# Last block of a three-block transformer step: index keys and attention keys and values projected as one tile of 328 columns, and another table of hooks

## The reference, cut to what matters

```python
SPLITS = (ATTN_WIDTH, KV_WIDTH, KV_WIDTH, IDX_HEADS * IDX_DIM, IDX_DIM, IDX_HEADS, D_RNN, D_RNN, D_MODEL, D_MODEL)
#         q 512       k 128     v 128     qi 512               ki 64    wi 8       xr 1024 yr 1024 gate_a   gate_b
dots = jnp.einsum('bqhd,bsd->bqhs', qib, k_idx) * (IDX_DIM ** -0.5)
score = jnp.einsum('bqh,bqhs->bqs', wb * (IDX_HEADS ** -0.5), jax.nn.relu(dots))
_, sel = lax.top_k(where(causal, score, -inf), n_sel)          # 64 of 256 keys for each query
logits = q . k[sel] + rel_bias ; p = softmax(logits) ; o = p @ v[sel]     # 8 heads, 2 key/value heads
rnn = rg_lru(conv(xr), w_rg, b_rg, w_ig, b_ig, lru_lambda) * gelu(yr)     # linear recurrence over 256 steps
merged = sigmoid(gate_a) * dot(attn, w_o_attn) + sigmoid(gate_b) * dot(rnn, w_o_rnn)
```

## Time and profile before

| | us |
|---|---|
| median of 3 runs | 1084.23 (1083.28 to 1085.28) |
| the profiled execution | 1086.36 |
| its span, first to last instruction | 1084.3 |
| TensorE matmul busy | 1026.4 (95%) |
| VectorE busy | 732.6 (68%) |
| ScalarE busy | 585.8 (54%) |
| GpSimd busy | 115.6 (11%) |
| DMA | 213.98 MB, mean 197 GB/s |

### The profile page before, as it was taken

The page is one execution under the profiler, slowest core; times in us unless marked ns, Lnnn a source line. Parts: engine busy times, 40 slices in busy tenths (PEclk is TensorE's granted clock), DMA queues, the critical chain, the costliest instruction groups (busy, mean ns, idle before and its releaser), DMA issues.

```text
span 1084.3 us, 13459 instructions
## 1 busy us (share of the span) xinstructions
PE 1026.4 (95%) x5180; PEld 850.1 (78%) x5180; DVE 732.6 (68%) x986; ACT 585.8 (54%) x842; POOL 115.6 (11%) x168
## 2 busy tenths in 40 slices
PE   6897999999999989899999999997999999999996
PEld 4675878889888777788888878886877788888885
DVE  5567775566346577578888666769766765777753
ACT  6657554444335567544443354577656456676641
POOL 0112140000000022200000011013630000000001
PEclk9999999999999999999999989999999999999998
DMA  9765479555556432389999796535465535554431
GB/s 348 274 170 73 136 202 303 188 181 174 194 175 197 157 113 76 101 287 352 353 325 320 295 317 215 166 121 165 147 213 206 163 112 184 191 193 156 175 136 39
DMA packets 98190, 213.98 MB, mean 197 GB/s; under 512 B 5440, under 2 KB 12880, under 8 KB 94736
## 3 DMA queue, kind: packets, MB, share of 16 engines
q1 hardware_dynamic: 93424, 196.39, 53.2%
q0 software_dynamic: 4416, 16.51, 6.3%
q10 hardware_dynamic: 288, 0.23, 0.1%
HBM read 208.39 MB, written 6.15 MB: 198 GB/s over the span
## 4 chain that ended last, share of the span: by engine, by line
PE 73%; DVE 11%; ACT 8%; issue 4%; DMA 2%; POOL 1%; SPq 0%; DVEq 0%; ACTq 0%; POOLq 0%
PE bank L883 22%; PE bank L885 22%; PE bank L884 22%; ACT hi L1199 4%; DVE lo L1634 4%; PE bank L861 3%; PE bank L898 1%; PE bank L863 1%; ACT junk L1062 1%; DMA raw<-in_w_in_a 1%; DVE early L1465 1%; DVE xres L1508 1%; DMA raw<-in_w_gate_up 1%; DMA early<-in_memT 1%; PE bank L944 0%
## 5 line engine op out<-in xcount | busy, mean ns | idle before, releaser
L1634 DVE TENSOR_TENSOR lo<-raw,hi 128x2048 fp32r<-128x2048 f32 (+1 forms) x164 | 366.9, 2240 | 215.7 <-ACT hi L1199 215.1
L1199 ACT ACTIVATE hi<-raw 128x2048 fp32r<-128x2048 f32 (+1 forms) x164 | 303.7, 1855 | 184.2 <-PE bank L885 144.0
L883 PE MATMUL bank<-hi,xTh 128*128 128x512 f32 (+2 forms) x896 | 346.8, 387 | 2.6 <-DVE lo L1634 2.2
L885 PE MATMUL bank<-hi,xTl 128*128 128x512 f32 (+2 forms) x896 | 337.7, 377 | 0.0
L884 PE MATMUL bank<-lo,xTh 128*128 128x512 f32 (+2 forms) x896 | 337.7, 377 | 0.0
L883 PEld LDWEIGHTS bank<-hi,xTh 128*128 128x128 f32 x896 | 170.6, 190 | 33.7 <-DVE lo L1634 2.8
L885 PEld LDWEIGHTS bank<-hi,xTl 128*128 128x128 f32 x896 | 170.2, 190 | 31.7
L884 PEld LDWEIGHTS bank<-lo,xTh 128*128 128x128 f32 x896 | 170.5, 190 | 28.5
L883 PE MATMUL bank<-hi,hTh 128*128 128x512 f32 x264 | 103.5, 392 | 0.2 <-DVE lo L1634 0.2
L885 PE MATMUL bank<-hi,hTl 128*128 128x512 f32 x264 | 102.8, 389 | 0.0
L884 PE MATMUL bank<-lo,hTh 128*128 128x512 f32 x264 | 102.8, 389 | 0.0
(11 more groups left out here) (346 smaller groups left out, 1315.2 us busy)
## 6 DMA issues: line engine op xcount, KB each, us to landing
raw<-in_w_gate_up SPq DMA_DIRECT2D x44, 1024.0 KB, 6.4
raw<-in_w_down SPq DMA_DIRECT2D x30, 1024.0 KB, 5.1
raw<-in_w_ada SPq DMA_DIRECT2D x24, 1024.0 KB, 6.2
raw<-in_w_up SPq DMA_DIRECT2D x22, 1024.0 KB, 5.1
raw<-in_w_in SPq DMA_DIRECT2D x21, 1024.0 KB, 5.0
raw<-in_w_out SPq DMA_DIRECT2D x12, 1024.0 KB, 5.1
raw<-in_w_in_b SPq DMA_DIRECT2D x10, 1024.0 KB, 5.1
raw<-in_w_in_a SPq DMA_DIRECT2D x6, 1024.0 KB, 11.9
```

The source lines that it names most:

```text
L883: e.matmul(o, sh, h[:, k, :], start=p.first and k == 0, stop=False)
L885: done = e.matmul(o, sl, h[:, k, :], start=False, stop=p.last and k == p.nk - 1)
L1199: e.activation(hi_s[m % SPLITS][:, 0:n], raw[p.at % RAWS][:, 0:n], ACT.Copy).then_inc(hi_made, 1)
L1634: e.tensor_tensor(lo_s[s][:, 0:n], raw[p.at % RAWS][:, 0:n], hi_s[s][:, 0:n].bitcast(F), ALU.subtract).then_inc(lo_made, 1)
```

## The change

**One tile for two.** The tiles `kw` (index key and index weights, 72 columns, second in the table) and `kv` (keys and values, 256 columns, eighth) become one tile `kvw` of 328 columns, second in the table. The host reorders the columns of `w_in_2` and `b_in_2`, so that they are neighbours. The copies that doubled the keys for two heads of a pair (lines 1589 and 1595) are gone: the bias additions read their operand twice. The index key gets its own buffers, those of the first probability slot. Transposes `ki` and `kv` now wait for the whole bias addition of `kvw`.

**Another table of hooks.** The steps behind the queries' tile are laid over four tiles instead of five. `scan0` and `scan1` come later relative to the tiles, `rec1` comes ahead of `top6` and `top7`, `half1` and `bias1` come ahead of `s2`.

```diff
-IN2 = [("qi", 768, 512, ["", "", ""]),
-       ("kw", 1280, 72, ["qi0", "qi2", "x1"]),
-       ("xr", 1352, 512, ["ki", "h0", ""]),
+IN2 = [("qi", 512, 512, ["", "", ""]),
+       ("kvw", 1024, 328, ["qi0", "qi2", "x1"]),
+       ("xr", 1352, 512, ["ki", "h0", "kv"]),
        ("yr", 2376, 512, ["conv00", "h2 conv02", "h4"]),
        ("xr", 1864, 512, ["gelu00", "gelu02 h6", "gate000 gate002 top"]),
        ("yr", 2888, 512, ["gate010 gate012 top0", "conv10 top1", "rec0"]),
-       ("q", 0, 512, ["conv12 top2", "gelu10 inc0 top3", "gelu12 scan0"]),
-       ("kv", 512, 256, ["top4", "half0 bias0 q0 gate100 top5", "q2 gate102 gate110 gate112"]),
-       ("gb", 4424, 512, ["kv top6 top7", "rec1 mask", "attend inc1 s0"]),
-       ("gb", 4936, 512, ["s1 scan1", "s2", "half1 bias1"]),
-       ("ga", 3400, 512, ["", "s3", "s4"]),
-       ("ga", 3912, 512, ["s5", "s6", "s7"])]
+       ("q", 0, 512, ["conv12 top2", "gelu10 inc0 top3", "gelu12 top4"]),
+       ("gb", 4424, 512, ["scan0 q0", "half0 bias0 q2 gate100 gate102", "top5 gate110 gate112"]),
+       ("gb", 4936, 512, ["rec1 top6 top7", "mask attend inc1", "scan1 s0"]),
+       ("ga", 3400, 512, ["s1", "half1 bias1 s2", "s3"]),
+       ("ga", 3912, 512, ["s4", "s5", "s6 s7"])]
...
+        kiT = [x[:, 0, :] for x in p_slots[2][0]]
...
                 elif kind == "ki":
-                    e.wait_ge(kw_dup, 2)
-                    turned(claim(step), blocks_of(staged2_slot("kw"), 128, 1))
+                    e.wait_ge(acc_dve, in2_tile[1024].d1)
+                    turned(claim(step), blocks_of(staged2_slot("kvw"), 384, 1))
                 elif kind == "kv":
-                    e.wait_ge(kv_dup, 4)
-                    turned(claim(step), blocks_of(staged2_slot("kv"), 256, 2))
+                    e.wait_ge(acc_dve, in2_tile[1024].d1)
+                    turned(claim(step), blocks_of(staged2_slot("kvw"), 0, 2))
...
-                elif kind == "in2" and l == "kv":
-                    s = staged2_slot("kv")
+                elif kind == "in2" and l == "kvw":
+                    s = staged2_slot("kvw")
                     e.wait_ge(acc_dve, t_.d1)
-                    e.activation(v[2][0][:, :, :], s[:, :, 128:256], ACT.Copy).then_inc(v2_high, 1)
+                    e.activation(v[2][0][:, :, :], s[:, :, 256:384], ACT.Copy).then_inc(v2_high, 1)
...
-                if what == "kw":
-                    e.wait_ge(acc_dve, t_.d1)
-                    e.tensor_scalar(wi[:, :, :], s[:, :, 64:72], 8.0 ** -0.5, None, ALU.mult).then_inc(wi_made, 1)
-                    for u in range(2):
-                        e.tensor_copy(s[:, :, 128 + 64 * u:192 + 64 * u], s[:, :, 0:64]).then_inc(kw_dup, 1)
-                elif what == "kv":
...
+            def project_keys(t_, pair, full, s, row):
+
+                def twice(x, heads):
+                    return x.rearrange("p (h d) -> p h d", h=heads).unsqueeze(2).to_broadcast([128, heads, 2, 64])
+
+                for t in range(2):
+                    e.wait_ge(*full[t])
+                    e.tensor_tensor(s[:, t, 384:512].rearrange("p (h u d) -> p h u d", h=1, u=2), twice(pair[t][:, 256:320], 1), twice(row[:, 256:320], 1), ALU.add)
+                    e.tensor_tensor(wi[:, t, :], pair[t][:, 320:328], row[:, 320:328], ALU.add).then_inc(wi_sum, 1)
+                    e.tensor_tensor(s[:, t, 0:256].rearrange("p (h u d) -> p h u d", h=2, u=2), twice(pair[t][:, 0:128], 2), twice(row[:, 0:128], 2), ALU.add)
+                    e.tensor_tensor(s[:, t, 256:384], pair[t][:, 128:256], row[:, 128:256], ALU.add).then_inc(acc_dve, 1)
+                e.wait_ge(wi_sum, 2)
+                e.tensor_scalar(wi[:, :, :], wi[:, :, :], 8.0 ** -0.5, None, ALU.mult).then_inc(wi_made, 1)
+                e.wait_ge(v2_high, 1)
+                e.tensor_tensor(v[2][1][:, :, :], s[:, :, 256:384], v[2][0][:, :, :].bitcast(F), ALU.subtract).then_inc(v2_low, 1)
```

More of the change, by code:

```diff
@@ L431, in named @@
     def named(self, name):
-        for kind in ("conv", "gelu", "qi", "ki", "kv", "top", "half", "bias", "rec", "inc", "scan", "gate", "q", "h", "s"):
-            if name.startswith(kind) and name not in ("kv", "ki", "top"):
+        for kind in ("conv", "gelu", "qi", "top", "half", "bias", "rec", "inc", "scan", "gate", "q", "h", "s"):
+            if name.startswith(kind) and name != "top":
                 numbers = tuple(int(x) for x in name[len(kind):])
@@ L605, in build @@
             sem(n) for n in ("mod_made", "gain_made", "gates_made", "norm_dve", "norm_act", "z_made", "z_high", "z_low", "x1_made"))
[L606 to L607 removed]
+        row_made, wi_sum, wi_made, v2_high, v2_low, head_added, mask_made, masked = (
+            sem(n) for n in ("row_made", "wi_sum", "wi_made", "v2_high", "v2_low", "head_added", "mask_made", "masked"))
         ig_x, decay_made, tanh_made, sq_made, mult_made, root_m, inc_made, scanned, rnn_made, r_high, r_low = (
@@ L1018, in tensor_program @@
                         e.wait_ge(*emptied(("ki",)))
-                    scores([("ihead", h), ("ihead", h + 1)], [(half_of(qy[2], h_), half_of(kT[2], h_, 0)) for h_ in (h, h + 1)], 128)
+                    scores([("ihead", h), ("ihead", h + 1)], [(half_of(qy[2], h_), [y[64 * (h_ % 2):64 * (h_ % 2) + 64, :] for y in kiT]) for h_ in (h, h + 1)], 128)
                 elif kind == "conv":
@@ L1288, in scalar_program @@
                 elif kind == "ki":
-                    high_of(step, kT[2][0][:, 0:1, :], two(x_bank(step), 1), 1.0)
+                    high_of(step, kiT[0], x_bank(step)[:, 0:256])
                 elif kind == "kv":
@@ L1533, in evacuate @@
                     e.wait_ge(x_full, filled(end_of[before]))
-                    if before == "kw":
-                        e.wait_ge(wi_made, 1)
+                    if before == "kvw":
+                        e.wait_ge(v2_low, 1)
                     e.wait_ge(*full[1])
@@ L1581, in project @@
                 e.wait_ge(d_brow[n % 2], 16 * (n // 2 + 1))
+                row = gbc[:, n % 2 * 512:n % 2 * 512 + w]
+                if what == "kvw":
+                    return project_keys(t_, pair, full, s, row)
                 for t in range(2):
                     e.wait_ge(*full[t])
-                    e.tensor_tensor(s[:, t, 0:w], pair[t][:, 0:w], gbc[:, n % 2 * 512:n % 2 * 512 + w], ALU.add).then_inc(acc_dve, 1)
-                if what == "kw":
-                    e.wait_ge(acc_dve, t_.d1)
-                    e.tensor_scalar(wi[:, :, :], s[:, :, 64:72], 8.0 ** -0.5, None, ALU.mult).then_inc(wi_made, 1)
-                    for u in range(2):
-                        e.tensor_copy(s[:, :, 128 + 64 * u:192 + 64 * u], s[:, :, 0:64]).then_inc(kw_dup, 1)
-                elif what == "kv":
-                    e.wait_ge(v2_high, 1)
-                    e.tensor_tensor(v[2][1][:, :, :], s[:, :, 128:256], v[2][0][:, :, :].bitcast(F), ALU.subtract).then_inc(v2_low, 1)
-                    for t in range(2):
-                        for u in range(2):
-                            e.tensor_copy(s[:, t, 256:512].rearrange("p (h u d) -> p h u d", h=2, u=2)[:, :, u, :],
-                                          s[:, t, 0:128].rearrange("p (h d) -> p h d", h=2)).then_inc(kv_dup, 1)
@@ new lines, in project @@
+                    e.tensor_tensor(s[:, t, 0:w], pair[t][:, 0:w], row, ALU.add).then_inc(acc_dve, 1)
+            def project_keys(t_, pair, full, s, row):
[9 more added lines that the diff above has]
+                e.tensor_scalar(wi[:, :, :], wi[:, :, :], 8.0 ** -0.5, None, ALU.mult).then_inc(wi_made, 1)
+                e.wait_ge(v2_high, 1)
+                e.tensor_tensor(v[2][1][:, :, :], s[:, :, 256:384], v[2][0][:, :, :].bitcast(F), ALU.subtract).then_inc(v2_low, 1)
@@ L1753, in vector_program @@
                 elif kind == "ki":
-                    h, lo = kT[2]
-                    low_of(step, lo[:, 0:1, :], two(x_bank(step), 1), h[:, 0:1, :], 1.0)
+                    low_of(step, kiT[1], x_bank(step)[:, 0:256], kiT[0])
                 elif kind == "kv":
@@ L2105 @@
     given = {n: np.ascontiguousarray(v) for n, v in inputs.items()}
+    for name in ("w_in_2", "b_in_2"):
+        x = given[name]
+        given[name] = np.ascontiguousarray(np.concatenate([x[..., 0:512], x[..., 768:1280], x[..., 512:768], x[..., 1280:]], axis=-1))
     given["constants"] = shape_constants()
```

13 lines of the change are left out of this document (6 added, 7 removed).

## The result

The changed kernel takes 1096.8 us (median of four runs, 1095.9 to 1098.3), the kernel before 1084.8 (four runs, 1083.3 to 1085.7). The ratio is 1.0112, with a 95% interval of 1.0096 to 1.0128: slower by 12.0 us. The forecast was 1096.0. The profiled execution after took 1095.9, with a span of 1093.8.

What follows compares the result with a forecast made beforehand. TensorE held 73% of the chain, but some waits were bound by short steps between engines. The terms gave 12.8 us lost, or 12.0 by waits; taking 12, 1086.4 became 1098.4, less 2.1: 1096, range 1087 to 1103.

Steps and rivals of the forecast that it cites:

- The tile: On TensorE, matmuls of the two old tiles (5.4 + 5.8 us) give way to the joined tile's (7.2): 3.9 us gained.
- The clock behind 72 columns: On TensorE at 665 to 670: the clock's fall after the run of 72-column matmuls goes, 1.5 us gained.
- The key: At the index key: two new TensorE waits, 1.9 us for its addition and 2.1 for its `lo`, 4.0 lost.
- The queries: At the queries' transposes: TensorE waits 3.4 us for their bias addition in place of 4.0, 0.6 gained.
- The recurrence: Second half's recurrence, through head 0's scaling on GpSimd: the step chain ends 10.3 us later, plus 0.3 of transposes, 10.6 lost.
- The sum: Whole change: 12.8 us lost by following the chain, 12.0 by counting waits; 12 taken.
- The waits behind head 0: At the scalings of heads 4 and 6: two waits of about 2.0 us for one of 1.8, 2.2 more.
- the wait ahead of the second part of `ga`: In the first `ga` tile: TensorE stands 2.6 us for a split that waits behind the mask.
- the rival that I gave 0.15: The clock falls at the waits of 1.9 to 2.6 us too, each costing 1.5: 17 lost, 1101; chance 0.15.
- The rival of the slack: The chain has slack, only direct terms count, if i times x ends by about 759: 1080 us; chance 0.07.
- The rival of the shorter chain: Early `gb` addition, or head 0's softmax done before `half1`: 5 to 8 us lost instead of 12, 1091; chance 0.20.

Runs made afterwards that it cites:

- e6: Joined tile with a new order of steps, key and queries turned later, the bias row behind `rec1`, against the kernel before: 1071.8 us, ratio 0.9867.
- e8: The two old tiles with a new order of steps, `rec1` within the first `gb` tile, against the kernel before: 1077.3 us, ratio 0.9922.
- e2: The two old tiles with the changed kernel's order of steps behind the queries' tile, against the kernel before: 1098.2 us, ratio 1.0119.
- e10: Changed kernel with the index key turned one chunk later and the first index scores two chunks later: 1093.6 us, ratio 1.0064 to the kernel before.
- e3: Changed kernel with top-k rounds 6 and 7 ahead of `rec1`: 1094.8 us, ratio 1.0080 to the kernel before.
- e4: Changed kernel with GpSimd issuing the bias row that waits for the `gb` addition behind its `rec1` product: 1094.0 us, ratio 1.0067 to the kernel before.
- e9: Changed kernel with both the top-k rounds ahead of `rec1` and the bias row behind its product: 1092.5 us, ratio 1.0054 to the kernel before.
- e1: Joined tile alone, steps behind the queries' tile in their old sequence, against the kernel before: 1094.8 us, ratio 1.0079.

## Why the prediction was right

**The tile, 3.9 gained: right.** Of the 328-column matmuls, two within one chunk, eleven steps apart (1.64 / 11 = 0.149 us; 0.150 was taken from the earlier trace rows):

```profile
664.27 0.31 PE L885 MATMUL bank<-hi,xTh 128*128 128x328 f32 x1
...
665.91 0.31 PE L887 MATMUL bank<-hi,xTl 128*128 128x328 f32 x1
```

The stage without its waits (10.4 us before, 25.7 after) and without what the stretches of low clock cost (5.1 and 6.3) is 180.0 us before and 176.6 after, 3.4 less, and e6 against e8 gives 4.

**The clock behind 72 columns, 1.5 gained: right here, and not certain.** The counterparts of the earlier trace rows, after (busy TensorE, clock, DMA), 665, 740 and 795 to 805:

```profile
665.00:670.00 5.00, 3.97 (x21) 1.00 0.66 216
740.00:745.00 5.00, 2.35 (x8) 0.77 0.74 242
...
795.00:800.00 5.00, 5.00 (x14) 0.50 0.48 120
800.00:805.00 5.00, 5.00 (x31) 0.92 0.55 206
```

All eleven profiles with the joined tile show 1.00 at 665 to 670. With the old tiles two of three show a fall (the kernel before, and e8), e2 does not. So the gain is one of this pair of executions; with the old tiles it isn't lost every time. The row of e8:

```profile
665.00:670.00 5.00, 5.00 (x22) 0.68 0.51 153
```

**The key, 4.0 lost: right, a little less.** Waits of 1.5 and 1.8 for 1.9 and 2.1 predicted; e10, where they are gone and all behind them comes 3.7 sooner, shows that they count in full.

**The queries, 0.6 gained: right.** The addition ended 90.2 us from the zero, in the clock of the profile before 745.9; predicted 746.2. The wait was 3.3 for 3.4.

**The recurrence, 10.6 lost: right in its links, 9.2 measured.** In the same clock, predicted and measured: product of the first half 753.2 and 752.9; `gb` addition 764.8 and 764.2; product of i and x 769.5 and 768.6; `L1813` 775.0 and 774.0; mask 778.9 and 777.7; product of `inc` 785.8 and 784.4; GpSimd's product behind the second scan 790.6 and 789.3; scaling of head 0 799.3 and 798.2. The error grows to 1.4 in small steps of the same sign; I laid the links end to end without any overlap, and which of them were too long I didn't take apart. The long wait ends 9.2 later than the wait it was set against (142.6 and 133.4), where I had 10.3. e3, e4 and e9 show that the two links (top-k rounds, bias row) are in the chain, and e1 that the row's wait comes with the joined tile even when the old sequence is kept. On this point the step had the right answer and too small a role for its reason: I named the row as one link among many.

The prediction compares head 0's scaling after with head 1's before. Head 0's own is 17.8 us later (124.7 and 142.5). By GpSimd's product behind the second scan 9.8 of them are there (123.9 and 133.7), and 8.1 come behind it, where `half1` and the DMAs of `bias1` stand ahead of that scaling; e2, in which the product is in time, has the same 8. In e1, with these steps in their old sequence, the scaling ends 3.2 us behind that product, where it is 8.9 in the changed kernel, and the rest up to `rTl` is as long (65.5 and 66.0). That suggests that this link counts too, but no run puts these steps back alone, so how much of the 12 us it holds is not shown.

**The sum, 12: right, with two errors that cancel.** The waits behind head 0 are 0.8 and 1.8, 2.6 in place of 4.0, and the wait ahead of the second part of `ga` is 1.3 in place of 2.6; the long one is 15.3 for 13.8. All waits together are 25.7 for 27.8, 2.1 less. Against it the clock: I had it give 1.5, and over the whole stage it costs 1.2 more than before. I took the stretch behind the long wait as it was before. But behind 15.3 us of idling the granted clock is 0.50 in the stretch 795 to 800 (the lower level, 1.2 GHz) and 0.92 in the next, 2.9 lost of the two stretches, where behind the 2.7 us wait of before it was 0.68 in the stretch 790 to 795, 1.6 lost. That the forecast of 1096.0 came within 0.8 us of the measurement is in part luck. And in the profile after the clock fell once more, behind the 1.8 us wait at 823:

```profile
825.00:830.00 5.00, 5.00 (x24) 0.69 1.03 396
```

This is the rival that I gave 0.15. It took place once in this profile, not three or four times, and costs 1.5 a fall. The rival of the slack fell with the result: i times x ended at 768.6 in the clock of the profile before, not by 759. The rival of the shorter chain named an early `gb` addition; it was 0.6 early, and the time of 1091 didn't come. Its other branch, the softmax of head 0 out of the way before `half1`, didn't happen either: ScalarE did it at 788.8 in the profile after, right ahead of `half1`'s `hi`.

## What to carry to other kernels

When a tile is joined to another and goes from a list, every step hooked behind it moves across the ends of other tiles, and each end has here a bias addition on VectorE and on GpSimd a wait for it and a DMA issue; write down for each engine what a step was ahead of and is now behind. On an engine that is busy a tenth of the time, one early DMA issue with a wait in front of it can be the costliest instruction of the change. What a late point costs is its own time plus the work left behind it, so predict when a wait ends, not how long it is.
